# Small experts: half of the tokens dense in plain float32, the other half by gathered rows of U and V

## The reference, cut to what matters

```python
q = (xt @ w_query).reshape(T, 8, 2, 128)                 # 8 heads, two halves
scores = einsum('thpc,hpnc->thpn', q, sub_keys)          # 128 scores for each half
top_s, top_i = top_k(scores, 16)
cand_s = top_s[:, :, 0, :, None] + top_s[:, :, 1, None, :]
best_s, best_pos = top_k(cand_s.reshape(T, 8, 256), 16)  # 16 of 256 pairs
idx = i * 128 + j of the chosen pairs;  gate = softmax(best_s)
# each token has 8 x 16 = 128 picks
act = gelu(einsum('cd,ced->ce', x, expert_u[idx]))       # expert_u: [16384, 1024]
y   = einsum('ce,ced->cd', gate * act, expert_v[idx])    # expert_v: [16384, 1024]
```

## Time and profile before

| | |
|---|---|
| Time, median of 3 runs | 3048.44 us (3046.49 to 3050.02) |
| The profiled execution | time 3049.45 us, span 3047.7 us |
| Busy share of the span: PE, PEld, DVE, ACT, POOL | 95%, 79%, 63%, 35%, 19% |
| Mean rate of all DMA | 188 GB/s |

### The profile page before, as it was taken

The page is one execution under the profiler, slowest core; times in us unless marked ns, Lnnn a source line. Parts: engine busy times, 40 slices in busy tenths (PEclk is TensorE's granted clock), DMA queues, the critical chain, the costliest instruction groups (busy, mean ns, idle before and its releaser), DMA issues. The chain is left out here.

```text
span 3047.7 us, 53137 instructions
## 1 busy us (share of the span) xinstructions
PE 2881.4 (95%) x20756; PEld 2415.8 (79%) x20756; DVE 1927.2 (63%) x3006; ACT 1056.5 (35%) x1582; POOL 569.7 (19%) x337
## 2 busy tenths in 40 slices
PE   8989889999977999989999999989999899999997
PEld 8978755555435888877999999987888789999997
DVE  5786442111003558877788888755498778888887
ACT  4533311000002532334444444435223444444443
POOL 0012101111100000000444444300000024444442
PEclk9999999999998999999999999999999999999999
DMA  7400239999997234225555555470341355555553
GB/s 220 151 19 3 93 156 397 419 418 419 419 419 260 77 104 149 80 80 170 192 181 191 184 188 188 170 260 28 132 157 51 117 180 187 185 189 183 191 181 144
DMA packets 186329, 573.99 MB, mean 188 GB/s; under 512 B 22066, under 2 KB 88114, under 8 KB 161216
## 3 DMA queue, kind: packets, MB, share of 16 engines
q1 hardware_dynamic: 182480, 567.60, 50.9%
q0 software_dynamic: 3696, 4.21, 0.4%
HBM read 612.64 MB, written 11.27 MB: 205 GB/s over the span
## 5 line engine op out<-in xcount | busy, mean ns | idle before, releaser
L2666 POOL TENSOR_TENSOR u_low<-u_raw,u_top 128x1024 fp32r<-128x1024 f32 x192 | 464.7, 2420 | 1615.7 <-ACT u_top L2575 1615.7
L2488 PE MATMUL psum<-v_top,hid 128*128 128x512 f32 x1888 | 621.5, 392 | 7.2 <-DVE hid L2773 7.2
L2488 PE MATMUL psum<-h_parts,u_top 128*128 128x256 f32 x3072 | 561.2, 283 | 4.6 <-DVE h_parts L2816 4.6
L2488 PEld LDWEIGHTS psum<-h_parts,u_top 128*128 128x128 f32 x3072 | 492.2, 192 | 20.2 <-DVE h_parts L2816 5.5
L2782 DVE TENSOR_TENSOR hid<-gelu,hid 128x256 fp32r<-128x256 f32 x192 | 479.2, 2496 | 6.5
L2488 PE MATMUL psum<-h_parts,u_low 128*128 128x256 f32 x1536 | 435.3, 283 | 0.0
L2488 PEld LDWEIGHTS psum<-v_top,hid 128*128 128x128 f32 x1888 | 356.2, 189 | 79.9 <-issue 9.5
L2488 PE MATMUL psum<-v_low,hid 128*128 128x512 f32 x944 | 370.3, 392 | 0.0
L1741 PE MATMUL psum<-piece_raw,tile_cols 128*64 128x256 f32 x2496 | 290.5, 384 | 17.9 <-DMA piece_raw<-w_up_dram 8.3
L2592 ACT ACTIVATE v_top<-v_raw 128x1024 fp32r<-128x1024 f32 x192 | 203.5, 1060 | 285.3 <-PE psum L2488 285.3
L2488 PEld LDWEIGHTS psum<-h_parts,u_low 128*128 128x128 f32 x1536 | 294.8, 192 | 0.0
(11 more groups left out here) (534 smaller groups left out, 4464.6 us busy)
## 6 DMA issues: line engine op xcount, KB each, us to landing
v_raw<-expert_v_dram SPq DMA_DIRECT2D x236, 512.0 KB, 3.5
u_raw<-expert_u_dram SPq DMA_DIRECT2D x192, 512.0 KB, 4.2
piece_raw<-w_gate_dram SPq DMA_DIRECT2D x78, 1024.0 KB, 18.5
piece_raw<-w_up_dram SPq DMA_DIRECT2D x78, 1024.0 KB, 14.4
piece_raw<-w_down_dram SPq DMA_DIRECT2D x78, 1024.0 KB, 23.9
in_raw<-w_in_dram SPq DMA_DIRECT2D x48, 1024.0 KB, 5.2
all_gates<-expert_u_dram SPq DMA_DIRECT2D x64, 512.0 KB, 3.5
query_raw<-w_query_dram SPq DMA_DIRECT2D x16, 1024.0 KB, 6.9
```

Source lines behind the costliest of these rows:

```text
L2488: last = nc.tensor.matmul(out, r32(lhs[i]), r32(rhs[j]), start=start and n == 0, stop=stop and n == 2, skip_group_check=True)
L2666: nc.gpsimd.tensor_tensor(r32(low_u[:, k, :]), raw_u[:, k, :], top_u[:, k, :], ALU.subtract).then_inc(u_low_done, 1)
```

## The change

Tokens 0 to 127 ("dense") keep the way over all 128 blocks, but in plain float32 with no splits: `dense` is eight matmuls of 128 columns a block, `back` is two of 512. 72 blocks are done ahead (44 beside the selection, 28 beside the spreading of now 16 groups), and 56 in the loop. Four `stay_busy` matmuls are added to each of the 128 turns of the loop. Tokens 128 to 255 ("sparse"), now selected first, get their 128 picks one at a time: GpSimd gathers, for pick c, the row of U of each token (128 rows of 4 KB, 512 KB in all) into a ring of eight buffers, and VectorE multiplies it by the token's x, kept in two banks of PSUM, and sums. ScalarE applies Gelu to the 128 sums, and the same is done with the rows of V, each scaled and added up in the same two banks. These 256 gathers a layer are shared out in VectorE's order: two beside each group of one-hots, the other 224 over the 128 turns of the loop. A row-major copy of U is added to the inputs. The rings for the dense loads are four blocks of U and seven of V.

```diff
-EARLY = 32
-RAW_E = 4
+EARLY = 72
+RAW_U, RAW_V = 4, 7
+RING = 8
-SPREAD = T // GROUP
+SPREAD = P // GROUP
...
+    N, E, PICKS = NKEYS, EARLY, PH * TOPK
+    DENSE, SPARSE = 0, 1
+    ORDER = (SPARSE, DENSE)
+    EXP_AFTER = (14, 38)
+    LISTS_AFTER = 44
+    BESIDE_HOTS = 2
+    LEAD = 8
+    FILL = 4
...
+        both = PS[:, 6:8, :].rearrange("p b c -> p (b c)")
...  SyncE
+                def load_u(n):
+                    if n >= RAW_U:
+                        sp.wait_ge(scored, n - RAW_U + 1)
+                    sp.dma_start(raw_u[:, n % RAW_U, :], ud(n)).then_inc(u_in[n % RAW_U], 16)
+                def load_v(n):
+                    if n >= RAW_V:
+                        sp.wait_ge(y_done, n - RAW_V + 1)
+                    sp.dma_start(raw_v[:, n % RAW_V, :], vd(n)).then_inc(v_in[n % RAW_V], 16)
...  TensorE
+                def dense(n):
+                    bank = (4 if n < E else 0) + n % 2
+                    pe.wait_ge(u_in[n % RAW_U], 16 * (n // RAW_U + 1))
+                    if n >= 2:
+                        pe.wait_ge(acted, n - 1)
+                    for c in range(KD):
+                        last = nc.tensor.matmul(PS[:, bank, 0:P], raw_u[:, n % RAW_U, c * P:(c + 1) * P], h_full[:, c, :],
+                                                start=(c == 0), stop=(c == KD - 1), skip_group_check=True)
+                    last.then_inc(scored, 1)
...
+                def back(n):
+                    pe.wait_ge(v_in[n % RAW_V], 16 * (n // RAW_V + 1))
+                    pe.wait_ge(gated, n + 1)
+                    for m in range(2):
+                        last = nc.tensor.matmul(PS[:, 4 + m, :], slot(n), raw_v[:, n % RAW_V, m * BANK:(m + 1) * BANK],
+                                                start=(n == 0), stop=(n == N - 1), skip_group_check=True)
...
+                for n in range(N):
+                    back(n)
+                    if E + n < N:
+                        dense(E + n)
+                    stay_busy(nc, S, 2, FILL)
...  GpSimd
+                pool.wait_ge(picks_known, 1)
+                for s in range(2 * PICKS):
+                    r, c = s % RING, s % PICKS
+                    if s >= RING:
+                        pool.wait_ge(picked_done, s - RING + 1)
+                    nc.gpsimd.indirect_dma_start(
+                        out=ring[:, r, :], out_offset=None, in_=S["u_rows"] if s < PICKS else S["v_rows"],
+                        in_offset=bass.IndirectOffsetOnAxis(ap=own_row[:, c:c + 1], axis=0),
+                        bounds_check=LAYERS * N * N - 1, oob_is_err=False).then_inc(row_in[r], 16)
...  VectorE
+                def gate(n):
+                    dve.wait_ge(acted, n + 1)
+                    tt(slot(n), slot(n), G[:, :, n], ALU.mult).then_inc(gated, 1)
+                def pick(s):
+                    r, c = s % RING, s % PICKS
+                    dve.wait_ge(row_in[r], 16 * (s // RING + 1))
+                    row = ring[:, r, :]
+                    if s < PICKS:
...
+                        nc.vector.tensor_tensor_reduce(row, row, both, 1.0, 0.0, ALU.mult, ALU.add,
+                                                       own_sum[:, c:c + 1]).then_inc(picked_done, 1)
+                        return
...
+                        stt(both, row, own_share[:, c:c + 1], both, ALU.mult, ALU.add).then_inc(picked_done, 1)
...
+                for g in range(SPREAD):
                     hots(g)
+                    for s in range(BESIDE_HOTS * g, BESIDE_HOTS * (g + 1)):
+                        pick(s)
...
+                for n in range(LEAD):
+                    gate(n)
+                before = BESIDE_HOTS * SPREAD
+                left = 2 * PICKS - before
+                for n in range(N):
+                    if n + LEAD < N:
+                        gate(n + LEAD)
+                    for s in range(before + n * left // N, before + (n + 1) * left // N):
+                        pick(s)
```

More of the change, by code:

```diff
@@ L2276, in one_row @@
     return S["dram"][name][bass.ds(layer, 1), :].rearrange("l n -> (l n)").partition_broadcast(P)
-EARLY = 32
-RAW_E = 4
+EARLY = 72
+RAW_U, RAW_V = 4, 7
+RING = 8
 GROUP = 8
-SPREAD = T // GROUP
+SPREAD = P // GROUP
 NC = TOPK + (TOPK - 1) * (TOPK // 2)
[L2286 to L2316, removed]
+UPPER_FLOATS = RAW_U * D + RING * D + KD * P + 4 * PH * TOPK
 def small_experts(nc, S, layer, spare, norm):
@@ L2403, in _ @@
             def _(sp):
[L2404 to L2441, removed]
@@ L2532, in _ @@
+                for n in range(LISTS_AFTER):
+                    dense(n)
+                turn_lists()
+                at_block = LISTS_AFTER
                 for g in range(SPREAD):
                     spread(g)
[L2534 to L2544 removed]
@@ L2545, in _ @@
-                hidden(E + 1, 1)
-                back(E, 0)
-                with pe.Fori(E // 2 + 1, PAIRS) as i:
-                    hidden(i * 2, 0)
-                    back(i * 2 - 1, 1)
-                    hidden(i * 2 + 1, 1)
-                    back(i * 2, 0)
-                back(N - 1, 1, closes=True)
+                    upto = LISTS_AFTER + (g + 1) * (E - LISTS_AFTER) // SPREAD
+                    for n in range(at_block, upto):
+                        dense(n)
+                    at_block = upto
@@ new lines, in _ @@
+                for n in range(LISTS_AFTER):
+                    gelu(n)
+                    if n in EXP_AFTER:
+                        turn = EXP_AFTER.index(n)
+                        eng.wait_ge(exp_ready, turn + 1)
+                        nc.scalar.activation(powers, powers, ACT.Exp).then_inc(exp_done, 1)
+                eng.wait_ge(lists_t, 1)
+                nc.scalar.activation(lists[:, :, :], PS[:, 3, :].rearrange("p (i t) -> p i t", t=P), ACT.Copy).then_inc(lists_out, 1)
+                at_block = LISTS_AFTER
@@ L2732, in select @@
                         step(last)
-                    for h, to in enumerate((rows[:, a, 0, :], second)):
+                    for h, to in enumerate((rows[:, 0, :], second)):
                         one, other = (picked[:, h, :, r:r + 1].rearrange("p c o -> p (c o)") for r in range(2))
```

389 lines of the change are left out of this document (127 added, 262 removed).

## The result

The changed kernel takes 2842.65 us (median of 4 runs, 2837.32 to 2845.26), the kernel before 3049.14 beside it: ratio 0.932, 95% interval 0.931 to 0.933. The prediction was 2912 with a range of 2820 to 3045. The profiled execution took 2837.32 us, its span 2835.4. Lines are those of the changed kernel from here on: `dense` L2418, `back` L2441, `stay_busy` L166, `gate` L2652, the gathers L2538, the picks of U L2661 and of V L2670.

The account below looks back on a forecast made before the run. DMA was taken to bound the changed expert parts: 674.5 us a layer, 1349 for two against 1486.7 before, 138 less, so 3049.45 - 138 gives 2912 us, range 2820 to 3045.

Parts of the forecast that it names:

- TensorE thus waits for the gathers by way of `gated`: In the loop, VectorE's gates stand before picks awaiting gathered rows, so `back` can't run over eight blocks ahead of the picks.
- paid out of those waits: In the loop's later turns, the stay_busy matmuls, 221 us a layer, fit into time TensorE would spend waiting anyway.
- would come on the path if DMA were fast: Warning for the loop: the stay_busy matmuls, 221 us a layer, would add to the time if DMA were fast.
- the rival: Gathers as cheap as dense loads, 1.29 us; TensorE bounds the loop at 542 us; time around 2832; chance 18%.
- the 46% of DMA: Main case: DMA bounds the expert parts at 1.45 to 1.75 us a gather; 2912, range 2865 to 2980; chance 46%.
- A group: One group of one-hots before the loop: TensorE 4.92 us, VectorE with two picks 5.27, DMA 5.50, which was taken.
- The second rival: VectorE dearer, at 2.50 us a pick, or VectorE and GpSimd shutting each other out; 2980 to 3020 us; chance 14%.
- Left for the loop are 216 x 1.62 + 177 x 1.29 = 578 us: DMA time of a layer's loop: 216 gathers at 1.62 us and 177 dense loads at 1.29 us.
- the price of the middle: Gather cost of 1.62 us, from the 324 GB/s moved in the middle of four gathers in the earlier trace.
- DMA share near 1: Sign expected in the profile after: DMA share near 1 and 370 GB/s or so in the whole loop.
- 674.5: Sum for a layer in us: lateness 3, groups 88, last spread, copy and first gate 3.5, loop 578, close 2.
- covered, thinly: Beside selection, U's four buffers give a load 5.4 us against 4.2 to landing; if not enough, the lists come late.

Follow-up runs that it names:

- experiment 1: Changed kernel with no stay_busy matmuls in the loop's turns (FILL = 0 in place of 4); 2796.31 us, ratio 0.916 to the kernel before.
- experiment 4: Changed kernel without the loop's loads of U and V, so the gathers have the DMA engines to themselves there; 2839.88 us (one run).
- experiments 5: Changed kernel with three stay_busy matmuls a turn in place of four; 2797.58 us, ratio 0.917 to the kernel before.
- 10: Changed kernel with two stay_busy matmuls a turn and the Gelu of the sums moved from behind dense block E + 50 to E + 46; 2794.58 us, ratio 0.917.
- 12: Changed kernel with two fills, Gelu of the sums behind E + 46, and picks spread over the first 120 turns in place of 128; 2797.44 us, ratio 0.917.
- experiment 3: Changed kernel without the 256 gathers, the 256 picks and the Gelu of their sums, leaving the dense half; 2823.78 us (one run).
- Experiment 2: Changed kernel with each layer's first 8 gathers held back, one after every third dense block from block 22; 2838.53 us, ratio 0.930.
- 5 to 7: Changed kernel with three, two and one stay_busy matmuls a turn in place of four; 2797.58, 2796.31 and 2794.96 us.

## Why the prediction came out as it did

**Right range, wrong bound.** The step that failed is "TensorE thus waits for the gathers by way of `gated`": in the changed kernel `back` never waits for `gated`, and its 538.7 us are TensorE's own instructions, the `stay_busy` matmuls among them. Those the prediction had "paid out of those waits", with the warning that they "would come on the path if DMA were fast". That happened. That the time lies in the range is owed to the rival, which had 18% against the 46% of DMA.

**What was right.** The part bounded by TensorE before was found, and so was the count of what replaces it. The prediction's price of a loop without waits was 542 us; `back` takes 538.7. A group was put at 4.92 us for TensorE and 5.27 for VectorE; the 16 groups with the first gates took 1336.5 - 1253.4 = 83.1 us, about 5.0 each. A pick was put at 1.31 us: of U it takes a step of 1.14 (1.22 long, and the reading of the sum, 0.08, runs under the next); of V it is 1.29 long, but back to back there is one each 1.38 us (13 in 17.99 us at the end of experiment 1's first layer). A gathering instruction occupies GpSimd for 0.99 us, as in the earlier trace rows. VectorE and GpSimd did not shut each other out: the groups' stretch shows VectorE at 69.80 of 70 us beside 29 gathers, and the 16 `hot_i` of the layer, with both inputs in SBUF, last 1.216 to 1.226 us, about the 1.23 of the earlier trace rows. The second rival falls with that. Its sum had a slip: with 2.50 us a pick the loop would not have stayed hidden, since VectorE's 128 x 0.40 + 224 x 2.50 = 611 us are more than the 578 of DMA. Between these two the place of the second source made no difference: L1872 takes 1.28 us with both in SBUF, L2670 1.29 us with one of them in PSUM.

**The term that was mis-sized** is the gather in "Left for the loop are 216 x 1.62 + 177 x 1.29 = 578 us". A gather costs the engines 1.28 us in the stream (409 GB/s in the loop for gathers and loads together, 408 GB/s with the gathers alone in a stretch of experiment 4). With that the prediction's own formula gives 393 x 1.28 = 503 us, experiment 1 measured 497.5 for `back`, and the loop's bound passes to TensorE's 538. The 324 and 277 GB/s of the earlier trace rows were read as a rate. They are those of four transfers, of which the first had nothing ahead of it, and each of the four took 4.3 to 6.0 us from issue to landing. The prediction said that a full stream has no such ends and still took the price of the middle. That a few transfers move less because their time holds this latency is my reading, which no run tests by itself; what the runs show is 324 GB/s for four and 408 for a stream, in which a gather takes 7.1 to 7.9 us to landing (experiment 4, 1380 to 1420) and one is issued each 1.31.

**The signs.** "DMA share near 1" was named as the sign of the predicted bound, and it came (1.03), under the rival. It does not tell the two apart where the transfers may run ahead: the sign that did was TensorE without waits and a loop of 542 us, which the prediction also named. My expectations for experiments 5, 10 and 12 failed in the other direction: they counted on gains from the order of the work where the bytes were the bound.

**Smaller terms.** In the kernel before, the first layer's selection lasted 85.2 us (1153.9 to 1239.1). In the changed one the layer norm comes 722.8 us after the start of selection (1152.3 to 1875.1), which leaves 637.6 us for what was predicted at 674.5: up to the first one-hot 15.9 in place of 3, groups, copy and first gate 83.1 in place of 91.5, loop and close 538.6 in place of 580. The rival's sum was 634.5, and so near by luck in part: 12.9 us too little lateness stand against 4.4 too much in the groups and 5.4 too much in loop and close. The 12.9 us of lateness more go with the warning that was written and not priced ("covered, thinly"). `dense` up to the lists:

```profile
L2418 PE MATMUL psum<-all_gates x699: 275/275/550, 1158.6 to 1249.9; 128*128 128x128 f32 x175
its engine sat idle before it (us, times) until:
  DMA all_gates<-expert_u_dram: 8.0, 9
  issue: 6.4, 2
  ACT act L2489: 6.0, 1
```

It waited 8.0 us for U's loads and 6.0 once for ScalarE, while the first gathers were issued. In experiment 3, without gathers, it still waited 9.5 us for U's loads, and the first one-hot came 93.7 us after the start of selection in place of 101.1: 5.5 of the 12.9 us were there without any gather, and 7.4 come with them. Experiment 2 shows that their spacing hardly matters. Why ScalarE itself stood still once in each layer at that point (8.3 and 6.2 us) remains open; in experiments 1 and 2 that wait was absent, and the first one-hot came only 2.7 and 3.2 us less late in the first layer.

**What stays open.** The best kernels here lie at 2794 to 2797 us. That bytes bound them is argued and not shown: the loop moves 409 GB/s throughout, and neither less work on TensorE (experiments 1 and 5 to 7) nor VectorE's stall or order (10 and 12) changes the time, but no run took bytes away from a kernel with fewer fills. And DMA is full only from the groups on. With two fills it moves 272 GB/s from 1150 to 1200, 328 from 1200 to 1250 and 138 from 1250 to 1260, and four of the seven buffers of V are first filled behind the groups (in the changed kernel three loads of V are issued by 1166.3 and none more before 1336). Whether loads moved into those stretches would help at the same bytes was not tried either.

## What to carry to other kernels

The rate read from four transfers (324 GB/s) was a fifth below that of the stream (408 and 409); for a stream take the rate of the fullest stretch in the trace, whatever queue it came from, and keep the short one as the bound. A DMA share of 1 is no proof of a DMA bound when transfers run ahead (1.03 here beside a TensorE without a wait): look for a stretch in which the engines empty and see whether the suspected victim speeds up. Filler work that was paid out of waits can come onto the critical path once the real work beside it shrinks, so its right size is to be found again after each such change: here one matmul a turn less gave 42 us between the profiled executions (2837.32 to 2795.17) and 45 between the medians.

## What was unexpected in the hardware

- Row gathers from GpSimd's queue (128 rows of 4 KB) mixed with plain loads from SyncE's queue move 409 GB/s, as much as the gathers alone (408 in a stretch of experiment 4) and the loads of U alone (407 in the earlier trace rows).
- Filler matmuls were not needed to keep the time: without them the granted clock was 0.94 in the second layer's loop and 0.84 from 1700 to 1800, so part of the work ran at a lower clock (0.50 from 1750 to 1755; matmuls of up to 1221 ns in place of 592), and the kernel took 2796 us as with one, two or three fills at 0.99 to 1.00.
- The product with a running sum (L2661, one operand in PSUM) has a step of 1.14 us for 1024 columns (1255.69 to 1256.83), the same as the plain product for the one-hots (1.15 and 1.13, 1253.41 to 1254.56 to 1255.69), and the reading of its sum takes 0.08 us and starts together with the next pick, at 1256.83.
